# The order of the first modulation: scale weights ahead of shift weights, and the shift's product inside the first tile of the first feed-forward

## What is computed

```python
m  = jnp.split((jax.nn.silu(c)     @ w_mod[l] + b_mod[l])[:, None, :], 9, axis=-1)
mc = jnp.split( jax.nn.silu(c_ctx) @ w_mod[l] + b_mod[l],              9, axis=-1)
h  = h  + 0.5 * m[2]  * swiglu(modulate(rms_norm(h,  norm_ffn1[l]), m[0],  m[1]),  ffn1_w_gu[l], ffn1_w_down[l])
hc = hc + 0.5 * mc[2] * swiglu(modulate(rms_norm(hc, norm_ffn1[l]), mc[0], mc[1]), ffn1_w_gu[l], ffn1_w_down[l])
# modulate(x, shift, scale) = x * (1 + scale) + shift
# rms_norm(x, gain) = x * rsqrt(mean(x * x) + 1e-6) * gain
# swiglu(x) = (silu(gate) * up) @ w_down, where gate and up are the halves of x @ w_gu
```

## Time and profile before

| | |
|---|---|
| median of three runs | 3538.3 us (3537.45 to 3539.41) |
| profiled execution | 3538.13 us |
| its span in the trace | 3536.4 us |
| PE busy | 3360.7 us, 95% |
| DVE busy | 1865.8 us, 53% |
| ACT busy | 1164.5 us, 33% |
| POOL busy | 421.9 us, 12% |
| DMA | 263.49 MB, mean 75 GB/s |

### The profile page before, as it was taken

One profiled execution on the slowest core, in us unless ns is written; L12 is line 12 of the kernel. 1 busy time (PEld: TensorE's weight loads), 2 busy tenths in 40 slices (PEclk: granted clock), 3 DMA queues, 4 the chain that ended last, 5 costly groups with the idle time before them and its releaser, 6 DMA issues. The chain is left out here.

```text
span 3536.4 us, 69053 instructions
## 1 busy us (share of the span) xinstructions
PE 3360.7 (95%) x28748; PEld 2882.3 (82%) x28748; DVE 1865.8 (53%) x2801; ACT 1164.5 (33%) x1778; POOL 421.9 (12%) x286
## 2 busy tenths in 40 slices
PE   6999999999878899999999999999998978889999
PEld 5888888885658878888888888888885668779897
DVE  4552554664765555544554552554644755555353
ACT  3321322226652233322222331222226633244231
POOL 2000002004313210000001000002004333120000
PEclk9999999999999999999999999999999999999999
DMA  5222222440000012222221332221430000022222
GB/s 201 94 96 71 89 92 67 147 147 30 2 17 3 4 54 78 100 90 70 97 86 56 101 100 66 95 92 52 149 113 30 2 18 3 15 84 91 93 89 95
DMA packets 68278, 263.49 MB, mean 75 GB/s; under 512 B 7552, under 2 KB 8704, under 8 KB 67456
## 3 DMA queue, kind: packets, MB, share of 16 engines
q1 hardware_dynamic: 67664, 256.95, 21.7%
q10 hardware_dynamic: 432, 3.88, 0.3%
HBM read 258.70 MB, written 2.10 MB: 74 GB/s over the span
## 5 line engine op out<-in xcount | busy, mean ns | idle before, releaser
L240 PE MATMUL ps<-hn_hi,w_hi 128*128 128x512 f32 (+1 forms) x3520 | 872.0, 329 | 16.0 <-DVE hn_lo L446 5.9
L240 PE MATMUL ps<-hn_hi,w_lo 128*128 128x512 f32 (+1 forms) x3520 | 873.0, 329 | 0.0
L240 PE MATMUL ps<-hn_lo,w_hi 128*128 128x512 f32 (+1 forms) x3520 | 868.5, 328 | 0.0
L217 ACT ACTIVATE w_hi<-raw 128x1024 fp32r<-128x1024 f32 (+1 forms) x300 | 338.6, 1129 | 1387.5 <-PE ps L240 1233.2
L222 DVE TENSOR_TENSOR w_lo<-raw,w_hi 128x1024 fp32r<-128x1024 f32 (+1 forms) x300 | 396.8, 1323 | 468.9 <-ACT w_hi L217 460.8
L240 PEld LDWEIGHTS ps<-hn_hi,w_hi 128*128 128x128 f32 x3520 | 547.6, 190 | 83.3 <-issue 17.6
L240 PEld LDWEIGHTS ps<-hn_lo,w_hi 128*128 128x128 f32 x3520 | 547.7, 190 | 61.4
L240 PEld LDWEIGHTS ps<-hn_hi,w_lo 128*128 128x128 f32 x3520 | 544.3, 189 | 61.2
L240 PE MATMUL ps<-g_hi,w_hi 128*128 128x512 f32 (+1 forms) x1424 | 397.9, 347 | 6.8 <-DVE g_lo L880 6.8
L240 PE MATMUL ps<-g_lo,w_hi 128*128 128x512 f32 (+1 forms) x1424 | 403.6, 351 | 0.0
L240 PE MATMUL ps<-g_hi,w_lo 128*128 128x512 f32 (+1 forms) x1424 | 397.4, 347 | 0.0
(11 more groups left out here) (272 smaller groups left out, 4236.1 us busy)
## 6 DMA issues: line engine op xcount, KB each, us to landing
raw<-wgu SPq DMA_DIRECT2D x176, 512.0 KB, 3.6
w_mod_one<-wmod SPq DMA_DIRECT2D x109, 512.0 KB, 3.6
raw<-wdn SPq DMA_DIRECT2D x64, 704.0 KB, 4.1
raw<-win SPq DMA_DIRECT2D x44, 512.0 KB, 4.5
w_mod_two<-wmod SPq DMA_DIRECT2D x19, 512.0 KB, 5.6
w_mod_first<-wmod_first SPq DMA_DIRECT2D x4, 2048.0 KB, 23.0
raw<-wout SPq DMA_DIRECT2D x16, 512.0 KB, 3.5
h<-xT ACTq DMA_DIRECT2D x1, 3072.0 KB, 10.2
```

The lines of the kernel that those rows point to most:

```text
L217: act.activation(w_hi[s][:, 0:kt, :].rearrange("p k n -> p (k n)"), raw[s][:, 0:kt * P], ACT.Copy).then_inc(hi_ready[s].sem, 1)
L240: mm = pe.matmul(out[:, o:o + b - a], w[:, k, :], m[:, k, a:b], start=(k == 0 and w is w_hi[s] and m is mov_hi), stop=(k == kt - 1 and w i ...
```

## The change

It does five things.

- The order of the four modulation loads becomes scale (j 8 to 11, 12 to 15), then shift (0 to 3, 4 to 7). Block 0 of the feed-forward's weights goes between the first and the second; block 1 and the two shift loads are issued in the feed-forward's block.
- On ACT's queue `small` and `consts` come first and `h` last, with a semaphore of its own; the others wait for four loads only.
- `setup()` keeps silu(c) and its spreading. The products, copies, folds and biases of the modulation go into the first block of `ffn`, in two halves: the scale's ahead of block 0's product, the shift's between block 0's and block 1's.
- POOL's squares of `h` move from `setup()` into the first block of `ffn`, behind the barrier.
- The first pair of blocks is multiplied in another way: block 0 over 768 columns only; block 1 over 768 columns for k = 0 to 2, then `sums_pe`, then k = 3 and 4; then block 0 over the two shift columns, block 1 for k = 5 to 7, block 1 over the two shift columns.

The diff, cut to its core (bookkeeping of semaphores left out):

```diff
-        w_mod_first = at("w_mod_first", [P, MOD_FIRST, D_MODEL], R_N)
-        mod_row_first = at("mod_row_first", [P, MOD_FIRST * P], R_T - MOD_FIRST * P * 4)
+        w_mod_first = at("w_mod_first", [P, MOD_FIRST, D_MODEL], R_G)
+        mod_row_first = [gate[:, 0:512], tanh_g[:, 0:512]]
...
+        FIRST_LOADS = ((8, 12), (12, 16), (0, 4), (4, 8))
+        FIRST_BANKS = (2, 3, 4, 6)
+        FOLD_BANKS = (7, 7, 4, 4)
...
+        def first_stripes(pe, g):
+            pe.wait_ge(mod_first_loaded[g].sem, 16)
+            stripe_products(pe, ps[:, FIRST_BANKS[g], :], ...
+        def first_fold(pe, g):
+            pe.wait_ge(mod_copied.sem, g + 1)
...
+        def first_copy(dve, g):
+            dve.wait_ge(mod_first_ready.sem, g + 1)
+            dve.tensor_copy(mod_row_first[g % 2], ps[:, FIRST_BANKS[g], :]).then_inc(mod_copied.sem, 1)
...
+        def first_squares(pool):
+            pool.wait_ge(h_loaded.sem, 16)
+            pool.tensor_tensor(sum_sq[:, 0:NT], h[:, 0, :], h[:, 0, :], ALU.mult).then_inc(first_summed.sem, 1)
+            for k in range(1, KD - 1):
+                pool.tensor_tensor(h_sq[:, :], h[:, k, :], h[:, k, :], ALU.mult).then_inc(first_squared.sem, 1)
...
+                pool.tensor_tensor(sum_sq[:, 0:NT], sum_sq[:, 0:NT], h_sq[:, :], ALU.add).then_inc(first_summed.sem, 1)
...
                 def _(sp):
                     sp.dma_start(c_raw[:, :], A["cT"]).then_inc(setup_loaded.sem, 16)
                     sp.dma_start(cols_all[:, :, :], A["cols"]).then_inc(setup_loaded.sem, 16)
...
+                    first_load(sp, 0)
+                    first_raw(sp, 0)
+                    first_load(sp, 1)
+                    sp.wait_ge(setup_loaded.sem, 64)
...
                 def _(act):
-                    act.dma_start(h[:, :, :], A["xT"]).then_inc(setup_loaded.sem, 16)
+                    act.dma_start(small[:, :], A["small"]).then_inc(setup_loaded.sem, 16)
                     act.dma_start(const[:, :, :], A["consts"]).then_inc(setup_loaded.sem, 16)
-                    act.dma_start(small[:, :], A["small"]).then_inc(setup_loaded.sem, 16)
-                    act.wait_ge(setup_loaded.sem, 80)
+                    act.dma_start(h[:, :, :], A["xT"]).then_inc(h_loaded.sem, 16)
+                    act.wait_ge(setup_loaded.sem, 64)
...
 ffn, SP:
+                    if fresh:
+                        first_raw(sp, 1)
+                        first_load(sp, 2)
+                        first_load(sp, 3)
 ffn, POOL:
+                    if fresh:
+                        first_squares(pool)
 ffn, ACT:
                         split_hi(act, 0, KD, 0)
-                        shifts_hi(act, l, part, nt)
+                        act.wait_ge(h_loaded.sem, 16)
+                        act.wait_ge(moda_ready.sem, moda_ready.at(2))
                         for k in range(KD - 1):
                             gained_hi(act, k, nt)
                     gained_hi(act, KD - 1, nt)
                     split_hi(act, 1, KD, 0)
+                    if fresh:
+                        shifts_hi(act, l, part, nt, None)
                     rstd_act(act, nt, True)
 ffn, DVE:
+                        split_lo(dve, 0, KD, 0)
+                        for g in range(2):
+                            first_copy(dve, g)
+                        first_finish(dve, 7, KD, 2 * KD, 2, 2)
                         norm_gains(dve, l, gain, part)
-                        shifts_lo(dve, l, part, nt)
-                        split_lo(dve, 0, KD, 0)
-                        for k in range(KD - 1):
-                            gained_lo(dve, k, nt, hn_hi_ready.at(k + 2))
-                    sums_dve(dve, nt, True)
-                    gained_lo(dve, KD - 1, nt, hn_hi_ready.at(KD + 1))
-                    split_lo(dve, 1, KD, 0)
+                        for k in range(KD):
+                            gained_lo(dve, k, nt, hn_hi_ready.at(k + 1))
+                        split_lo(dve, 1, KD, 0)
+                        for g in range(2, 4):
+                            first_copy(dve, g)
+                        dve.wait_ge(first_summed.sem, KD - 1)
+                        sums_dve(dve, nt, True)
+                        first_finish(dve, 4, 0, KD, 4, 4)
+                        shifts_lo(dve, l, part, nt, None)
 ffn, PE:
+                    def first_pair():
+                        slot = [psf[:, 0:1024], psf[:, 1024:2048]]
+                        for g in range(2):
+                            first_stripes(pe, g)
+                            first_fold(pe, g)
...
+                        products_of(0, slot[0], range(KD), 0, NT, hn_lo_ready)
+                        for g in range(2, 4):
+                            first_stripes(pe, g)
+                        for g in range(2, 4):
+                            first_fold(pe, g)
...
+                        products_of(1, slot[1], range(0, 3), 0, NT)
+                        sums_pe(pe, nt)
+                        products_of(1, slot[1], range(3, 5), 0, NT)
+                        pe.wait_ge(hn_lo_ready.sem, hn_lo_ready.at(KD + 1))
+                        products_of(0, slot[0], range(KD), NT, NTX).then_inc(block_done[0].sem, 1)
+                        products_of(1, slot[1], range(5, KD), 0, NT)
+                        products_of(1, slot[1], range(KD), NT, NTX).then_inc(block_done[1].sem, 1)
```

More of the change, by code:

```diff
@@ L324, in setup @@
         def setup():
-            n_setup = [0]
             with nc.Block() as block:
@@ L701, in gate_up, with products_of @@
                         product(pe, 1, KD, psf[:, 1024:2048], hn_hi, hn_lo, nt, spans=slot_spans(nt))
+                    def products_of(s, out, ks, a, b, tile_ready=None):
+                        for k in ks:
+                            if tile_ready is not None:
+                                pe.wait_ge(tile_ready.sem, tile_ready.at(k + 1))
+                            for w, m in ((w_hi[s], hn_hi), (w_hi[s], hn_lo), (w_lo[s], hn_hi)):
+                                for c, e in ((a, min(b, 512)), (512, b)) if a < 512 else ((a, b),):
+                                    mm = pe.matmul(out[:, c:e], w[:, k, :], m[:, k, c:e],
+                                                   start=(k == 0 and w is w_hi[s] and m is hn_hi),
+                                                   stop=(k == KD - 1 and w is w_lo[s]))
+                        return mm
```

106 lines of the change are left out of this document (49 added, 57 removed).

## The result

The changed kernel takes 3545.53 us (median; 3541.81 to 3550.32) where the kernel before took 3539.22 us on the same chip (3533.9 to 3541.45). By the medians it is 6.3 us slower; the ratio, over all runs of both kernels, is 1.0022 with a 95% interval of 1.0014 to 1.0030, which is 5 to 11 us. The forecast was 3542, with a change of less than 0.2% as the likeliest outcome. The measured 0.22% lies just beyond that, and its interval lies wholly above no change. The profiled execution took 3544.96 us, its span is 3543.2 us.

What follows compares the result with a forecast made beforehand. PE, busy 95% of the span, bounds the kernel, so only the first pair's end matters: 49.9 + 5.5 + 8.5 + 0.5 + 1.0 + 5.5 = 70.9 against 67.0, giving 3538.1 + 3.9 = 3542 us; range 3536 to 3547.

Steps and rivals of the forecast that it cites:

- the loads and the start: Before the first product: second scale load lands at 24.5 instead of 34.7, 10.2 us gained; feed-forward's block starts at 14.5.
- the lock, and where it bites: Gains and gained_lo before and in block 0: DVE and POOL alternate whole instructions, costing 4.4 us at the first tile.
- Rival 1: DVE and POOL do not hold each other up: block 0 ends at 43.9, time 3536.0; chance 0.20.
- what moves into PE's path: Between block 0 and block 1: the shift's two groups of stripes, 3.6 us, and two folds, 1.9; 5.5 together.
- The wait for POOL's squares: DVE's added wait before the shift's bias and lo part: already satisfied for 9 us.
- the narrow products: First pair: 48 new products of two moving columns at 0.115 us each, 5.5 us in all, 2.7 to 9.1.
- Rival 3: First pair: the two-column products take the full 0.19 us each, 3.6 us more, time 3545.6; chance 0.07.
- what follows is a stretch of PE work that starts when the first pair ends: After the first pair: PE stays busy, so the change moves the time only by moving that pair's end.
- the sum: End of the first pair: 49.9 + 5.5 + 8.5 + 0.5 + 1.0 + 5.5 = 70.9 us, 3.9 us later than before.
- the base: Profiled execution of the kernel before: first pair ends at 67.0 us, whole execution takes 3538.1 us.
- POOL starting late: Start: `small` and `consts` come at 14.3, POOL's squares run until about 49; 11 us later, 3549; chance 0.08.

Runs made afterwards that it cites:

- e1_no_squares: Changed kernel with POOL's squares of tiles 1 to 6 left out; 3542.66 us against 3536.99 for the kernel before, 1.0016.
- e2_no_narrow: Changed kernel without the 48 products of two moving columns in the first pair; 3538.92 us, 1.0005 of the kernel before.
- e8_halves: Changed kernel with both blocks of the first pair cut at column 512, the other 258 columns late; 3539.99 us against 3538.14 for the kernel before, 1.0002.
- e0_after: The changed kernel run again unedited, as reference; 3548.27 us against 3538.14 for the kernel before on the same chip, 1.0026.

## Why the prediction was right or wrong, point by point

**Right: the loads and the start.** Forecast: chain of silu(c) from 5, block at 14.5, second scale load at 24.5. Measured 6.30, 14.89 and, for the load, 25.1 (issued at 2.70, 22.4 us in flight). The stripes started at 25.58, since PE was at the first group's fold until then, at half clock. `h` landed at 15.7 and not 14.3, and POOL began there.

**Right: the lock, and where it bites; that the end of block 0 came so near is in part luck.** Forecast: gains done at 32.6, tile 0 ready at 37.0, tile 1 at 39.9, block 0 ending at 49.9. Measured: gains done at 33.3, products from 37.39 and 39.93, end 49.34. Rival 1 (3536, the lock isn't felt) falls by this trace and by `e1_no_squares`. Inside it terms were off and nearly cancelled. The stripes began 1.1 us later and took 3.59 us for 3.35, and the fold took 1.87 us at half clock where I took 1.0. Against that the two gains took 1.13 us where I had put 2.5, and the clock came back at 43.9 and not 45.7. One reading in that passage doesn't follow from its own figures: 14.4 us of POOL's work at 1.7 us each are 8 to 9 instructions and not 7 to 8; by 30.1 us nine had been started. The lock's size depends on how much of POOL's work is left when `gained_lo` starts: with POOL beginning at 15.71 they took 11.59 us, at 15.85 and 16.10 12.9, at 17.0 to 17.5 (three traces) 14.4.

**Right: what moves into PE's path.** Forecast 5.5 us for the shift's stripes and folds; measured 5.35. The wait for POOL's squares cost nothing, as forecast.

**Right in itself: the narrow products.** Forecast 0.115 us each, 5.5 in all; measured 2.6 us for each 24, 0.108 each, 5.2 in all. Rival 3 (0.19 each, 3545.6) comes out near the measured time, but for a reason that isn't there. The Trainium skill's 81 ns for sustained matmuls of 128 columns ("TensorE: Matmul & The Clock Gate", section "Back-to-back issue gap") does not hold here: products with a 128x128 weight load each follow at 0.11 us, with 2 columns as with 130.

**Wrong: that this is all they cost.** The step that failed is in the sentence at the start, "what follows is a stretch of PE work that starts when the first pair ends", and in the sum, which took block 1 as 8.5 us and the second pair at its old length. Both assume that a busy PE keeps its clock. Rows 5 show the clock low only behind idle stretches, and I took idle to be the only cause. Measured, two runs of 24 narrow products were each followed by 3.4 us at half clock, 3.3 us in all: block 1 with the sums took 11.4 instead of the 10.0 of the forecast, and the second pair 18.58 instead of 16.96 us. The first hides in the start of the second pair (71.31 against a forecast of 70.9, the sum's other errors being on the good side), the second lies behind it, where I had stopped looking. `e2_no_narrow` and `e8_halves` show the term from the other side: without narrow products 7.8 us go behind block 0 in the first, and 8.1 us at the mark against `e0_after` in the second, not 5.2.

**Wrong in size: the base.** The trace on which I built reached its third pair 1.0 us later than the mean of three. Against that mean the change is 7.5 us at the mark. So the forecast's own sum is a change of 4.9 us against that mean, not 3.9; a single trace could not have told me.

Together: forecast +3.9; 0.4 for the start of the second pair, 1.6 for the second pair's length, 0.9 for the rest of the kernel, which moves by as much without any change, make the 6.8 us of the two profiled executions (3538.13 to 3544.96). The range held the time; the chance of slower, 0.15, was too small, because its largest part hung on POOL starting late and nothing stood in it for the clock.

## What to carry to other kernels

Work that needs an operand late should be cut where a matmul ends anyway: a late remainder of 258 columns added no matmul and left the clock full, one of 2 columns cost 5.2 us for its 48 added products and 3.3 us in clock. Where work moves to a time in which DVE is on the path, look for what GpSimd does at that time; here the same squares on DVE, made while it waited for a load, were worth 3.2 us at the mark. And of a load brought forward by ten us, ask which of the engines behind it are free by then: here only three to five of them arrived on PE's path.

## What of the hardware was not expected

- PE's clock fell to 1.2 GHz although PE was never idle: for 3.4 us at or behind the end of the first run of 24 matmuls of 2 columns with 128x128 weights in all five traces that have such runs, and for 3.4 or 6.8 us at the end of the second in four of them. It did not fall with 24 of 130 columns at the same spacing (one trace), nor with the same 48 spread in groups of 3 to 12 between wide ones (one trace).
- The number of columns does not set the spacing of these products: 0.11 us with 2 columns and with 130. Each has a weight load of its own, recorded at 0.19 us at full clock as in rows 9; that the loads set the spacing is my reading, and no run takes them away.
- The lock of DVE and GpSimd goes by whole instructions and lasts as long as both have some left: sixteen `gained_lo` took 8.56 us alone, 11.6 beside three of POOL's instructions, 12.9 beside four, 14.4 beside five. The Trainium skill's rule of an exclusive lock on the port pair that the two share ("SBUF — State Buffer", section "Who interferes with whom") agrees.
- The modulation's stripes ran at half or full clock in traces of the same kernel: 3.35 us for sixteen behind an idle 3.12 us of PE, 1.90 behind an idle 0.43, by which alone the start moves 1.5 us.
